# The second pair's three mixers in a two-pair transformer kernel: an order of steps written out for each engine, and one product per level for keys and queries

## What is computed

```
h = rmsnorm_2(x, norm1_g[l]);  u = h @ w_in[l]         # 3592 columns, split:
# mq mk mv mo (256 each), mi mf (4 each); aq ak av (512 each); hq hf hi hg (256 each)
y_m = mlstm_mixer(...)      # causal conv + silu on q and k; gate rows by log-sigmoid, cumsum, running max;
                            # h = num / max(|den|, exp(-m)); rmsnorm per head; times sigmoid(mo)
y_a = diff_attention(...)   # q, k rmsnorm and rotary; two softmaxes per head, a = p0 - lam * p1; rmsnorm
y_h = hgrn2_mixer(...)      # silu(hq); f from sigmoid(hf); decays exp(cumsum log f); rmsnorm; times silu(hg)
x = x + concat(y_m, y_a, y_h) @ w_out[l]
x = x + square(relu(rmsnorm_2(x, norm2_g[l]) @ w_up[l])) @ w_down[l]
```

## Time and profile before

| what | us |
|---|---|
| median of 3 runs (2457.44 to 2468.75) | 2467.63 |
| the profiled execution, its own time | 2461.01 |
| its span | 2459.2 |
| TensorE busy | 2291.0 |
| VectorE busy | 1577.3 |
| ScalarE busy | 1372.6 |

### The profile page before, as it was taken

The page is one execution under the profiler, slowest core; times in us unless marked ns, Lnnn a source line. Parts: engine busy times, 40 slices in busy tenths (PEclk is TensorE's granted clock), DMA queues, the critical chain, the costliest instruction groups (busy, mean ns, idle before and its releaser), DMA issues.

```text
span 2459.2 us, 38773 instructions
## 1 busy us (share of the span) xinstructions
PE 2291.0 (93%) x16290; PEld 2118.6 (86%) x16290; DVE 1577.3 (64%) x2235; ACT 1372.6 (56%) x1906; POOL 20.0 (1%) x14
## 2 busy tenths in 40 slices
PE   6999998999999999998999999999769999878999
PEld 6989998999999899897888888788559998757999
DVE  4675545666575665463888888867646655754665
ACT  5764545554566643554777777766544445644443
POOL 0000000000000000000000000000000000000000
PEclk9999999999999999997999999999789999988999
DMA  6441234556554313351888888954114564412554
GB/s 230 151 132 35 87 103 155 170 177 189 157 168 160 99 40 96 108 170 68 320 297 304 305 305 310 315 183 142 52 41 148 176 202 146 133 35 78 165 187 137
DMA packets 111205, 398.12 MB, mean 162 GB/s; under 512 B 12336, under 2 KB 12336, under 8 KB 110768
## 3 DMA queue, kind: packets, MB, share of 16 engines
q1 hardware_dynamic: 111024, 395.58, 48.4%
HBM read 394.48 MB, written 1.05 MB: 161 GB/s over the span
## 4 chain that ended last, share of the span: by engine, by line
PE 66%; DVE 16%; ACT 10%; DMA 6%; issue 2%; POOL 0%; SPq 0%; DVEq 0%; ACTq 0%
PE ps L418 65%; DVE wlo L2015 6%; DMA raw<-stream 5%; ACT whi L1241 4%; ACT arena L1251 2%; DVE arena L2015 2%; DVE arena L2023 2%; DVE scr L2015 1%; ACT arena_r L1251 1%; ACT scr L1251 1%; DVE h L2015 1%; DVE scr L2023 1%; ACT rst L1251 1%; DMA CO<-const 1%; DVE arena L2259 0%
## 5 line engine op out<-in xcount | busy, mean ns | idle before, releaser
L2015 DVE TENSOR_TENSOR wlo<-raw,whi 128x1024 fp32r<-128x1024 f32 (+1 forms) x762 | 903.2, 1199 | 539.4 <-ACT whi L1241 527.7
L1241 ACT ACTIVATE whi<-raw 128x1024 fp32r<-128x1024 f32 (+1 forms) x762 | 781.1, 1035 | 342.7 <-PE ps L418 264.5
L418 PE MATMUL ps<-uh,whi 128*128 128x256 f32 (+1 forms) x2240 | 654.1, 292 | 12.2 <-DVE wlo L2015 3.7
L418 PE MATMUL ps<-ul,whi 128*128 128x256 f32 (+1 forms) x2240 | 634.2, 283 | 0.0
L418 PE MATMUL ps<-uh,wlo 128*128 128x256 f32 (+1 forms) x2240 | 634.0, 283 | 0.0
L418 PE MATMUL ps<-arena_r,whi 128*128 128x256 f32 x2720 | 485.5, 281 | 12.1 <-DVE arena_r L2015 8.6
L418 PEld LDWEIGHTS ps<-uh,whi 128*128 128x128 f32 (+1 forms) x2240 | 428.7, 191 | 25.8 <-issue 17.0
L418 PEld LDWEIGHTS ps<-ul,whi 128*128 128x128 f32 (+1 forms) x2240 | 428.7, 191 | 7.4 <-issue 6.8
L418 PEld LDWEIGHTS ps<-arena_r,whi 128*128 128x128 f32 x2720 | 415.2, 188 | 16.4 <-issue 6.5
L418 PEld LDWEIGHTS ps<-uh,wlo 128*128 128x128 f32 (+1 forms) x2240 | 428.2, 191 | 0.0
L418 PE MATMUL ps<-arena_r,wlo 128*128 128x256 f32 x1360 | 379.5, 279 | 0.0
(11 more groups left out here) (163 smaller groups left out, 1897.6 us busy)
## 6 DMA issues: line engine op xcount, KB each, us to landing
raw<-stream SPq DMA_DIRECT2D x694, 512.0 KB, 4.0
raw<-stream SPq DMA_DIRECT2D x64, 384.0 KB, 4.2
CO<-const SPq DMA_DIRECT2D x1, 2305.0 KB, 14.3
h<-xT SPq DMA_DIRECT2D x1, 1024.0 KB, 6.9
raw<-stream SPq DMA_DIRECT2D x4, 256.0 KB, 2.6
out<-h SPq DMA_DIRECT2D x4, 256.0 KB, 2.2
arena<-pT SPq DMA_DIRECT2D x2, 256.0 KB, 3.6
SM<-small SPq DMA_DIRECT2D x1, 464.0 KB, 3.1
```

What stands on the lines that cost most here:

```text
L418: return self.e.matmul(o, l, r, start=start, stop=stop, skip_group_check=True)
L1241: self.e.activation(M.whi[:, b:b + n], M.raw[:, a:a + n], ACT.Copy).then_inc(K.sem("weight_hi"), 1)
L2015: return self.e.tensor_tensor(o, a, b, op)
```

## The change

The three threads become more and smaller ones: the gate rows, the late gates (mo and hg) and the four group norms get threads of their own, and so do, on VectorE and ScalarE, the weight splits (`aheads`, 21 steps), the attention's rows, factors, maxima and turned copies, and hgrn's distances and masked copies. `turns` takes a string for each engine, and each letter of it runs the next step of one thread, so each engine has an order of its own (g gate rows, m mLSTM, a attention, h hgrn, l late gates, n norms, w splits, v lambda, p attention rows on ScalarE, r their factors or turns, x maxima, t copies of transposes, d distances, c masked copies). The norms come in the order 2, 0, 6, 4. Banks are dealt anew: 2 for mc, mo, hg and the norms' sums, 0 and 1 for the rest of the mLSTM, 3 to 5 attention, 6 and 7 hgrn.

For each level the distances are written into one of four 512-column parts of QK, the decay is made there, and one product of 512 columns multiplies the keys of the first half and the queries of the second half of each block (`ends` reads them from `hqk`, whose halves are swapped); TensorE reads keys and queries from the same tile. The attention's weights get a second buffer (`pa`, in the old place of hE), and its maxima and sums a set for each half of the queries. The mLSTM's reciprocal is made on ScalarE as Exp(-Ln(x)), and the maximum is one operation on 512 columns.

```diff
 DOUBLE = ("n1", 0)
-MLSTM = 4
+NORMS = (2, 0, 6, 4)
+TENSOR_B = "hhhgmhaaha aaaahggmga aaamamhall hamalmlmha mhahahnmha ahnaann"
+SCALAR_B = "wwhwhvwwgw hwwhpwwhpw hhhwpwrmwh grwwprwrmm wmhawwtlaw hltmtnmham nthnnanhtn ntnnnnn"
+VECTOR_B = "hwwhvwvgwg wwhwwchddw drdwwhwcgg dwgrrwrmrr wwwrrhmdcx mwhawcmxdw mawhhcdhch cxchmamnxn annnnnn"
...
         self.late = self.B["hg"][:, 0:384]
+        self.pa = [v3(self.B[x], 512) for x in ("pa", "hE")]
...
         m = self.co("lvl").bitcast(U8)[:, 2 * lev * P:2 * lev * P + P].rearrange("p (n s) -> p n s", s=2 * s)[:, :, s:2 * s]
         return m.unsqueeze(1).broadcast_to([P, 4, P // (2 * s), s])
 
+    def decay(self, lev):
+
+        return self.B["QK"][:, lev % 4 * 512:lev % 4 * 512 + 512]
+
+    def ends(self, lev):
+
+        x, s = self.B["hqk"], 1 << lev
+        return bass.AP(x.tensor, x.offset, [list(x.ap[0]), [2 * s, 256 // s], [512 + s, 2], [1, s]])
...
+
+    def turns(self, order, **threads):
+
+        for x in order:
+            if x != " ":
+                next(threads[x])
+        for x in threads.values():
+            assert next(x, "end") == "end"
...
+    def group_norms(self, l):
+
+        s, M = self.mark("tensor_norms"), self.M
+        for t0 in NORMS:
+            b = self.bank(self.ring((2,)), "fin", l, t0)
+            self.wait_ge(*self.K.when("fsq", l, t0))
+            self.mm(b, M.ones if 2 <= t0 < 6 else M.co("bones"), M.scr(self.K.slot("fsq", l, t0)), True, True).then_inc(
+                *s(("ps", "fin", l, t0), ("free", "fsq", l, t0)))
+            yield
 
...
-        self.level_scores(work, s, l, -1, v3(B["hqk"][:, 0:512]), v3(B["hqk"][:, 512:1024]))
-        yield
+        self.level_scores(work, s, l, -1, v3(B["hqk"][:, 512:1024]), v3(B["hqk"][:, 0:512]))
         yield
         for lev in range(8):
-            yield
-            yield
             self.wait_ge(*K.when("hqk", l, lev))
-            x = B["QK"][:, lev % 2 * 1024:lev % 2 * 1024 + 1024]
-            q, k = v3(x[:, 0:512]), v3(x[:, 512:1024])
-            self.level_scores(work, s, l, lev, q, k)
-            yield
-            if lev == 3:
-                yield from self.proj_T(work, s, ("hg", l), "w_in_2", l, 3336, 256)
+            x = v3(M.decay(lev))
+            self.level_scores(work, s, l, lev, x, x)
+            yield
...
-        yield from self.group_norm(work, s, l, 6, 2, M.co("bones"))
...
-        weave([self.mlstm(l), self.attention(l), self.hgrn(l)])
+        self.turns(TENSOR_B, g=self.gate_rows(l), m=self.mlstm(l), a=self.attention(l), h=self.hgrn(l), l=self.late_gates(l),
+                   n=self.group_norms(l))
...
+    def group_norms(self, l):
+
+        M, K, s = self.M, self.K, self.mark("scalar_norms")
+        scr = self.ring((5, 6))
+        for t0 in NORMS:
+            x, d = self.take(scr, "fsq", l, t0), M.B["mix"][:, t0 * T:(t0 + 2) * T]
+            self.wait_ge(*K.when(*{0: ("mraw", l), 2: ("ao", l, 0), 4: ("ao", l, 2), 6: ("ho", l)}[t0]))
+            self.act(x, d, ACT.Square).then_inc(*s("fsq", l, t0))
+            yield
+            self.rsq(self.rring((0,)), s, ("fin", l, t0), ("frs", l, t0), 512, 1.0 / (128 if 2 <= t0 < 6 else 64))
+            yield
+            self.wait_ge(*K.when("mixed tile", l, t0))
+            self.act(M.mixp[0][:, t0:t0 + 2, :], v3(d), ACT.Copy).then_inc(*s("mixh", l, t0))
+            yield
+
...
-        self.act(M.scr(K.slot("mden", l)), self.bank("md", l), ACT.Abs).then_inc(*s(("mden", l), ("free", "md", l)))
-        yield
-        yield from self.group_norm(scr, rst, s, l, 0, 2, 64, "mraw", l)
+        self.act(den, self.bank("md", l), ACT.Abs).then_inc(*s(("mden", l), ("free", "md", l)))
+        yield
+        self.ln_exp()
+        self.wait_ge(*K.when("mmax", l))
+        self.act(x, den, ACT.Ln).then_inc(*s())
+        self.wait_ge(*s.last)
+        self.act(x, x, ACT.Exp, scale=-1.0).then_inc(*s("minv", l))
+        yield
...
-        weave([self.mlstm(l), self.attention(l), self.hgrn(l)])
+        self.turns(SCALAR_B, w=self.aheads(21), g=self.gate_rows(l), m=self.mlstm(l), v=self.attention_lam(l),
+                   p=self.attention_rows(l), r=self.attention_norms(l), a=self.attention(l), t=self.attention_turned(l),
+                   h=self.hgrn(l), l=self.late_gates(l), n=self.group_norms(l))
...
+    def group_norms(self, l):
+        K, M, s = self.K, self.M, self.mark("vector_norms")
+        B, mix = M.B, M.B["mix"]
+        for t0 in NORMS:
+            d = mix[:, t0 * T:(t0 + 2) * T]
+            gain, times = {0: (M.sm("mlstm_norm_g_2", l)[:, 0:1], "mo"), 2: (B["cols"][:, 12:13], None),
+                           4: (B["cols"][:, 12:13], None), 6: (M.sm("hgrn_norm_g_2", l)[:, 0:1], "hg")}[t0]
+            self.wait_ge(*K.when("gs", l))
+            self.wait_ge(*K.when("frs", l, t0))
+            self.wait_ge(*K.when("fsq", l, t0))
+            q = self.stt(d, d, gain, self.rst("frs", l, t0), MUL, MUL)
+            if times:
+                q.then_inc(*s("free", "frs", l, t0))
+                self.wait_ge(*s.last)
+                self.wait_ge(*K.when(times, l))
...
-        em = self.scr("mem", l)
+        x = self.scr("mem", l)
         self.wait_ge(*K.when("mden", l))
-        for pt in range(2):
-            a = slice(pt * T, pt * T + T)
-            self.tt(den[:, a], den[:, a], em[:, a], MAX).then_inc(*s())
-            self.wait_ge(*s.last)
-            e.reciprocal(den[:, a], den[:, a]).then_inc(*s())
-        self.wait_ge(*s.last)
+        self.tt(den, den, x, MAX).then_inc(*s("mmax", l))
+        yield
+        self.wait_ge(*K.when("minv", l))
         self.wait_ge(*K.when("ps", "mn", l))
-        self.tt(B["mix"][:, 0:2 * T], den, self.bank("mn", l), MUL).then_inc(
+        self.tt(B["mix"][:, 0:2 * T], x, self.bank("mn", l), MUL).then_inc(
             *s(("mraw", l), ("free", "mn", l), ("free", "mden", l), ("free", "mem", l)))
...
+        yield
+        self.wait_ge(*K.when("hq", l))
+        self.wait_ge(*K.when("hk", l))
+        for lev in range(8):
+            sz = 1 << lev
+            E = M.decay(lev).rearrange("p (n h s) -> p n h s", h=2, s=sz)
+            self.wait_ge(*K.when("hE", l, lev))
+            self.tt(E, M.ends(lev), E, MUL).then_inc(*s("hqk", l, lev))
+            yield
...
+    def hgrn_decays(self, l):
+
+        K, M, s = self.K, self.M, self.mark("vector_decays")
+        for lev in range(8):
+            sz = 1 << lev
+            Bv = M.B["hB"].rearrange("p (n s) -> p n s", s=2 * sz)
+            mid = Bv[:, :, sz - 1:sz].broadcast_to([P, T // sz, 2 * sz])
+            self.wait_ge(*K.when("hB", l))
+            if lev > 3:
+                self.wait_ge(*K.when("ps", "hs", l, lev - 4, 1))
+            self.tt(M.decay(lev).rearrange("p (n s) -> p n s", s=2 * sz), Bv, mid, SUB).then_inc(*s("hE0", l, lev))
+            yield
...
+    def hgrn_scores(self, l):
+
+        K, M, s = self.K, self.M, self.mark("vector_scores")
+        for lev in range(-1, 7):
             for z in range(2):
-                d = v3(B["ST"][:, z * 1024:(z + 1) * 1024])[:, :, 0:P]
+                d = v3(M.B["ST"][:, z * 1024:(z + 1) * 1024])[:, :, 0:P]
                 b = v3(self.bank("hs", l, lev, z), P)
                 self.wait_ge(*K.when("ps", "hs", l, lev, z))
                 if lev < 0:
                     q = self.tt(d, b, wide(M.ident, P, 4), MUL)
                 else:
                     self.wait_ge(*K.when("hST", l, -1, z))
-                    q = e.copy_predicated(later(d, lev), M.meet(lev), later(b, lev))
+                    q = self.e.copy_predicated(later(d, lev), M.meet(lev), later(b, lev))
                 q.then_inc(*s(("hST", l, lev, z), ("free", "hs", l, lev, z)))
...
-        weave([self.mlstm(l), self.attention(l), self.hgrn(l)])
+        self.turns(VECTOR_B, w=self.aheads(21), g=self.gate_rows(l), m=self.mlstm(l), v=self.attention_lam(l),
+                   r=self.attention_rows(l), x=self.attention_max(l), a=self.attention(l), h=self.hgrn(l),
+                   d=self.hgrn_decays(l), c=self.hgrn_scores(l), n=self.group_norms(l))
```

More of the change, by code:

```diff
@@ L4 @@
 import numpy as np
-from concourse import mybir
+from concourse import bass, mybir
 ALU = mybir.AluOpType
@@ L1097, in normed @@
                 *s("ps", "asum", which, l, t))
-        pieces = chain(self.proj_T(work, s, ("aq", l), "w_in_2", l, 1032, 512),
-                       self.proj_T(work, s, ("ak", l), "w_in_2", l, 1544, 512))
-        for n, _ in enumerate(pieces):
-            if n % 2 and n > 1:
-                normed(n // 2 - 1)
-            yield
-        yield
-        normed(3)
+        yield from self.proj_T(work, s, ("aq", l), "w_in_2", l, 1032, 512)
+        ak = self.proj_T(work, s, ("ak", l), "w_in_2", l, 1544, 512)
+        for which, t in (("aq", 0), ("aq", 2), ("ak", 0)):
+            normed(which, t)
+            yield
+            for _ in range(2 if which == "aq" else 0):
+                next(ak)
+                yield
+        next(ak, None)
+        normed("ak", 2)
```

(53 more changed lines are left out.)

422 lines of the change are left out of this document (157 added, 265 removed).

## The result

The changed kernel takes 2380.89 us (median of 4 runs, 2380.02 to 2383.59), the kernel before 2466.74 beside it (4 runs, 2457.44 to 2468.75): ratio 0.9661, 95% interval 0.9635 to 0.9687. The profiled execution took 2380.11 us, its span is 2378.3. The forecast was 2386, range 2366 to 2413.

A forecast was written before the change was run, and what follows sets the result against it. Issue order was taken to bound the second half, TensorE's work what better order reaches. Stage 117.4 + 1.9 + 1.6 + 0.7 + 2.5 = 124.1 us, 75.1 less over two layers, from 2461.01 to 2386 us; range 2366 to 2413.

The forecast's parts named there:

- What bounds the kernel: Mixer stage: the order of steps bounds its second half; TensorE's work, some 105 us, bounds what better order reaches.
- w_out's slower start and fewer tiles ahead: After the mixers: 1.6 us for a clock of 0.67, 0.7 us for four tiles done ahead instead of six.
- their stall: Scores of level 1: due on TensorE at 59.5, their VectorE product ends at 61.2, a stall of 1.7 us.
- its stall: at21, the attention's transposes: wanted at 103.8, rows ready at 105.2 behind mixed2 and the exponentials, 1.4 us.
- tail, with the clock's part in its sums: Stage end after ao2: two norm chains one behind the other, 9.7 us, plus 1.9 us for two slow sums.
- hand-overs and small misses up to ao2's end: Whole stage: an estimate of 2.5 us for hand-overs of up to 0.14 us and small misses the walk omits.
- (a): Whole kernel: the forecast holds, 2370 to 2401 us, low end with no misses and a steady clock; chance 0.68.
- (b): From score 0 on: order stalls stay, 13 closely met steps each miss by 1 us, 2401 to 2425; chance 0.18.
- (c): Second half of the stage: clock stays at 0.76 despite work, 15 us more a layer, 2416 us; chance 0.06.
- (d): Whole stage: waits are true dependences, the same length in any order, no change, 2455 to 2467 us; chance 0.02.
- (e): Level products: the new access costs over 4.7 us more than 0.685 each, so the kernel is slower; chance 0.03.
- What leaves the other engines: Per layer: VectorE loses 4.3 us of products and 3.5 of reciprocals, leaving 89; ScalarE gains 1.3, reaching 85.

The follow-up runs named there:

- two-norms kernel: The changed kernel with the last norm (tiles 4 and 5) given a thread, bank and scale buffer of its own; 2371.74 us, ratio 0.9622.
- repeated run: The changed kernel without further edits, measured once more beside the later edits; 2384.11 us, ratio 0.9671.

## Why the prediction was right, step by step

**What bounds the kernel** was read rightly: the order. The old order in the new kernel brings all of the time back, and the kernels that change VectorE's volume move the medians by 4.3 us at most.

**The sum.** 2386 was predicted and 2380.1 is the profiled time it was made for: 5.9 us too many. In the predicted stage of 124.1 us stand 2.3 us (w_out's slower start and fewer tiles ahead) that fall behind the stage's end; the table sets them against what the spans behind the stages gained or lost. By its terms, layer 0, with t = 0 at 1672.51:

| term | predicted | measured |
|---|---|---|
| level 1's scores start | 61.2 | 62.8 |
| their stall | 1.7 | 1.8 |
| at21 starts | 105.2 | 105.9 |
| its stall | 1.4 | 1.1 |
| ao2 ends | 107.7 | 109.0 |
| tail, with the clock's part in its sums | 9.7 + 1.9 | 10.7 |
| w_out's slower start and fewer tiles ahead | 2.3 | 0.2; 2.4 in layer 1 |
| hand-overs and small misses up to ao2's end | 2.5 | 1.3 |

Both stalls were named with their places and sizes; a third, ao2's 0.78 us for the copy of at21, was in the walk's steps but not told as one. TensorE needed 61.0 us of work to level 1's scores where I had summed 59.5: the one place where the walk was short, and it was met by the estimate for misses. What was too dear is the clock. I took half the speed for both sums of the tail and 0.67 for the start of w_out. The first sum ran at full speed (1.10 us), behind waits of 1.12 and 0.78 us (in the kernel with the reciprocals on VectorE it took 1.91 us in layer 0 behind the same two, so this can go either way); only the last, behind 4.22 us of standing, was slow (2.04). The 4.74 us behind the stage were granted 1.00 in layer 0 and 0.61 in layer 1, so the term was right for one of the two. The stretch at 0.67 in the earlier trace rows lies inside the old stage; behind the old stages the same 4.74 us were granted 1.00 in both layers, which I had not looked up.

Two sizes of the prediction don't hold although the forecast does. TensorE's work was summed to some 105 us at full clock; the two-norms kernel's first stage, granted 1.00 throughout, has 108.9; 1.5 us a layer of the difference lie before level 1's scores, as above, and were met only by the estimate for misses. And the low end of (a), "no misses and a clock that holds", is 118.1 us a stage by the prediction's own terms, or 2374 us, not 2370. So the mechanism was right, and the closeness to 6 us is in part luck: work counted too low and terms for the clock and for misses set too high stood against each other.

**The rivals.** (b), order stalls: the 13 closely met steps missed by 1.3 us in all up to ao2's end, not by 13; the idle stretches above are all there are. (c), the clock low in the second half: the window from 1735.35 on was granted 0.94, all of its loss in the last 12 us (0.72 there, 1.00 before). Some of (c) can come, though, behind a short wait: in layer 1 the 3.1 us behind the 1.82 us of standing were granted 0.62, and the repeated run had 0.67 at that place in layer 0. That is some 1.5 to 1.7 us each time, for which the walk had no term. (d), true dependences: refuted, the stage is 41 us shorter. (e), the new access: level 0 pays 0.15 us, levels from 1 on nothing, against the 0.5 at two levels that I kept as the upper end. The Trainium skill (SBUF — State Buffer, "Door 1: The DMA port swizzle"), by which only level 0 should pay, named the level rightly, and the two runs' 0.83 against 0.68 agree with it; the size that I had taken from the masked copy (0.5) was over three times too large; that copy is another operation.

**What leaves the other engines.** Right in its numbers (VectorE 89 predicted, 90.4 measured; ScalarE 85 and 85.2). The text gave no gain to the reciprocal's move by itself. It has one, some 4 us in all, which the walk had in it without saying so: with the reciprocals ahead of them the weights of at20 are late by 2.06 us in each layer.

**What would have shown it wrong** didn't come: no wait of TensorE for `wlo` in the first half, no product near 1.2 us, no stage over 137 us, and a clock near 0.7 only in the tail (0.76 from 1780 to 1790, 0.69 from 2150 to 2160). The longest idle stretch before w_out lies in the last 10 us, as said; its 4.22 us were taken as part of a chain, and the two-norms kernel shows that 4.1 us of it were only ScalarE's order.

## What to carry to other kernels

Before counting an engine's work, see whether its idle time is made of waits for steps of other threads that merely stand ahead in a queue; if so, shortening those steps gives little (11 us of VectorE's work put back cost some 3) and moving them much (here some 84 us, which the old order takes back). Walk a proposed order with the durations of the trace, engine by engine, and write down the due time of each step: it named two of three stalls to 0.3 us, and the same walk shows what to move next (the last norm, 10 to 12 us). Where several stalls stand close together, removing the first mostly hands its time to the next one, so look for what is due right behind it first. And compare stages, not spans, when an effect is a few microseconds: in the profiles here layer 0's stage began anywhere from 1669.63 to 1678.62 us, behind the same untouched work, and in two cases that changed or hid what the edit did.

## What was not expected of the hardware

The granted clock behind the same steps came out in two ways in one run. The window of 1792.26 above has 1.00 in layer 0; the same 4.74 us in layer 1, and what follows them:

```profile
2160.44:2165.18 4.74, 4.74 (x26) 4.74 (x27) 2.13 (x3) 1.49 (x2) 0.00 (x0) 0.61 0.36 111
...
2165.00:2170.00 5.00, 5.00 (x45) 5.00 (x44) 1.72 (x3) 2.65 (x5) 0.00 (x0) 1.00 0.33 105
```

26 products in it instead of 40, so most of it ran at the lower of the two levels, 1.2 GHz instead of 2.4. In both layers the last sum (2.04 us instead of 1.10) and the tiles of w_out behind it ran at that level, behind 4.22 us of standing. In layer 0 the clock was back at the upper level when w_out went on at 1792.26; in layer 1 it came back only at 2163.8:

```profile
1786.87:1792.26 5.39, 4.60 (x14) 3.27 (x15) 1.36 (x4) 2.46 (x4) 0.00 (x0) 0.52 0.00 0
2155.05:2160.44 5.39, 4.60 (x14) 3.27 (x14) 1.36 (x4) 2.46 (x4) 0.00 (x0) 0.50 0.00 0
2160.44:2163.80 3.36, 3.36 (x15) 3.36 (x16) 1.51 (x2) 0.77 (x2) 0.00 (x0) 0.50 0.19 30
```

The repeated run had 1.00 behind both stages. In the two-norms kernel, which stands 2.05 us at most before w_out, the clock was 1.00 in the 10 us before w_out in both layers, and then 1.00 behind the first stage and 0.65 behind the second. There w_out went on at 2149.86 at full speed, and from 2151.0 to 2154.6 the clock was 0.54, though TensorE had no gap:

```profile
2149.86:2154.60 4.74, 4.74 (x27) 4.74 (x28) 2.74 (x3) 1.49 (x2) 0.00 (x0) 0.65 0.33 111
...
2145.35:2151.00 5.65, 3.60 (x23) 2.92 (x24) 4.30 (x8) 4.59 (x7) 0.00 (x0) 1.00 0.00 0
2151.00:2154.60 3.60, 3.60 (x20) 3.60 (x19) 1.78 (x2) 1.06 (x1) 0.00 (x0) 0.54 0.43 146
```

So the clock can stay low for some microseconds of full work behind a long wait, as in layer 1 of the changed kernel, and it can also fall a microsecond behind a shorter one, in work that fills TensorE, as here. Either is worth 1.7 to 1.9 us each time (4.74 us at 0.65 or 0.61 short of full speed), about as much as one of the stalls that the experiments moved, and two runs of one kernel differ by it.
